# Layer 0's 16 modulation slots between the pieces of the branches' merge in place of the route; GpSimd's third half there waits until the places are counted

## What is computed

```python
mod  = silu(c) @ w_ada[i] + b_ada[i]            # 6 x 1024 values, for x
modc = silu(c_ctx) @ w_ada[i] + b_ada[i]        # the same for the context
sh1, sc1, gt1, sh2, sc2, gt2 = split(mod, 6)
...
ga, gb, gc = split(sigmoid(gates), 3)
m = ga * (ya @ w_branch[0]) + gb * (yb @ w_branch[1]) + gc * (yc @ w_branch[2])
x = x + gt1 * (m @ w_out)                        # the merge, then "out"
h2 = modulate(rmsnorm(x, g_norm2[i]), sh2, sc2)
aff = softmax(h2 @ w_router)                     # 16 experts
gate, idx = top_k(aff^T, 32)                     # each expert takes 32 tokens
x = x + gt2 * experts(h2 gathered by idx)        # w_e1, w_e3, w_e2 per expert
```

## Time and profile before

| | us |
|---|---|
| median of 3 runs | 2873.31 |
| lowest, highest | 2867.41, 2874.86 |
| profiled execution | 2874.76 |
| its span in the trace | 2872.9 |
| PE busy in the span | 2546.1 (89%) |
| DVE, ACT, POOL busy | 1053.3, 882.9, 426.6 |
| merge and out of layer 0 | about 1197 to 1440 |
| route of layer 0 | about 1440 to 1506 |
| experts of layer 0 | about 1506 to 1970 |

### The profile page before, as it was taken

One profiled execution on the slowest core, in us unless ns is written; L12 is line 12 of the kernel. 1 busy time (PEld: TensorE's weight loads), 2 busy tenths in 40 slices (PEclk: granted clock), 3 DMA queues, 4 the chain that ended last, 5 costly groups with the idle time before them and its releaser, 6 DMA issues. The chain is left out here.

```text
span 2872.9 us, 37682 instructions
## 1 busy us (share of the span) xinstructions
PE 2546.1 (89%) x15020; PEld 1781.4 (62%) x15020; DVE 1053.3 (37%) x1526; ACT 882.9 (31%) x1395; POOL 426.6 (15%) x217
## 2 busy tenths in 40 slices
PE   7999989999999999799988888887897997888887
PEld 6888878899997678588842222224776983222222
DVE  4547633246754434544340011114455651000001
ACT  4565533344443344332331000002334441000001
POOL 0430017670000221100310000000232011000000
PEclk8999999999999999899989999999998998999999
DMA  5434327764543121322279999996212447999996
GB/s 212 162 133 162 118 77 302 295 229 161 183 151 130 59 70 45 147 103 92 99 310 410 421 421 421 421 421 262 103 60 84 174 176 328 422 421 421 421 421 272
DMA packets 92891, 669.49 MB, mean 233 GB/s; under 512 B 10288, under 2 KB 10432, under 8 KB 12736
## 3 DMA queue, kind: packets, MB, share of 16 engines
q1 hardware_dynamic: 90256, 654.63, 57.7%
q0 software_dynamic: 2208, 11.56, 1.1%
q10 hardware_dynamic: 272, 1.05, 0.1%
HBM read 666.13 MB, written 1.06 MB: 232 GB/s over the span
## 5 line engine op out<-in xcount | busy, mean ns | idle before, releaser
L2429 PE MATMUL ps<-ring,WK 128*64 128x512 f32 x2984 | 703.2, 604 | 116.0 <-DMA ring<-in_stream 91.6
L545 PE MATMUL ps<-A,piece_hi 128*128 128x256 f32 (+1 forms) x1952 | 621.0, 318 | 30.0 <-ACTq L442 7.2
L546 PE MATMUL ps<-A,piece_hi 128*128 128x256 f32 (+1 forms) x1952 | 607.7, 311 | 0.0
L547 PE MATMUL ps<-A,ring_lo 128*128 128x256 f32 (+1 forms) x1952 | 607.3, 311 | 0.0
L2429 PEld LDWEIGHTS ps<-ring,WK 128*64 128x64 f32 x2984 | 192.2, 137 | 591.2 <-DMA ring<-in_stream 284.5
L455 ACT ACTIVATE piece_hi<-ring 128x1024 fp32r<-128x1024 f32 x378 | 393.2, 1054 | 206.5 <-DVEq L571 105.2
L545 PEld LDWEIGHTS ps<-A,piece_hi 128*128 128x128 f32 x1952 | 380.0, 195 | 70.2 <-issue 36.8
L466 POOL TENSOR_TENSOR ring_lo<-ring,piece_hi 128x1024 fp32r<-128x1024 f32 x123 | 311.7, 2546 | 689.8 <-ACT piece_hi L455 689.6
L464 DVE TENSOR_TENSOR ring_lo<-ring,piece_hi 128x1024 fp32r<-128x1024 f32 x255 | 317.2, 1248 | 256.2 <-ACT piece_hi L455 255.7
L546 PEld LDWEIGHTS ps<-A,piece_hi 128*128 128x128 f32 x1952 | 380.5, 195 | 18.3
L547 PEld LDWEIGHTS ps<-A,ring_lo 128*128 128x128 f32 x1952 | 379.7, 194 | 18.3
(11 more groups left out here) (271 smaller groups left out, 2661.3 us busy)
## 6 DMA issues: line engine op xcount, KB each, us to landing
ring<-in_stream SPq DMA_DIRECT2D x610, 1024.0 KB, 11.7
WK<-in_ahead SPq DMA_DIRECT2D x5, 1024.0 KB, 11.6
WK<-in_na_bias POOLq DMA_DIRECT2D x2, 2048.0 KB, 8.0
hi_place<-in_ahead SPq DMA_DIRECT2D x4, 1024.0 KB, 13.9
WK<-cum_scratch POOLq DMA_DIRECT2D x1, 2048.0 KB, 10.8
A_place<-in_ahead SPq DMA_DIRECT2D x2, 1024.0 KB, 16.9
const<-in_const SPq DMA_DIRECT2D x1, 1235.0 KB, 10.4
WK<-in_x SPq DMA_DIRECT2D x1, 1024.0 KB, 5.1
```

The costliest lines, as they stand in the source:

```text
L545: nc.tensor.matmul(out_, l[0], r[0], start=first, stop=False)
L546: nc.tensor.matmul(out_, l[0], r[1], start=False, stop=False)
L547: return nc.tensor.matmul(out_, l[1], r[0], start=False, stop=last)
L2429: last = nc.tensor.matmul(ps[64 * n:64 * n + 64, bank, :], lhs, piece[:, n * 512:n * 512 + 512], start=(k == 0), stop=(k == DC - 1))
```

## The change

Layer 1's modulation slots 8 to 23 move, in the stream and in the programs of PE and DVE, from the route of layer 0 into its merge: one behind each of the first 16 pairs of pieces, with the turns of slots 8, 16 and 24. The merge of layer 0 rotates over banks 0 to 5, and `out` and the route over all 8. SyncE issues the four ahead loads behind the first six expert slots, where it did so 10 slots earlier in the stream. In the route POOL's subtraction for m = 2 also waits for `placed`; the one for m = 3 is queued behind it.

```diff
@@ _mark
         if layer == 0:
             steps(1, range(DC), 0)
-        at += MERGE_PIECES
-        if layer == 0:
-            steps(1, range(DC, 3 * DC), 0)
+            steps(1, range(DC, DC + 18), 2)
+            at += MERGE_PIECES - 36
+        else:
+            at += MERGE_PIECES
@@ merge_pe, merge_dve
-        def merge_pe(pe, cur, branches, kc, n, ada=None):
+        def merge_pe(pe, cur, branches, kc, n, ada=None, slot=0):
             yh, yl = y_split(kc, n)
-            slot = 0
@@ route_pe (and the same kind of lines in route_dve)
-            if ada:
-                ada_pe(pe, cur, 1, step[-1])
...
-                    if ada and at % 2 == 1 and at < 12:
-                        ada_pe(pe, cur, 1, 18 + at // 2)
@@ route_pool
                 pool.wait_ge(h2_hi, cur.base("h2") + m + 1)
+                if m == 2:
+                    pool.wait_ge(placed, cur.base("route") + 1)
@@ sync
-            run(R, EXPERTS_AT[0] // 2 - 4)
+            run(R, EXPERTS_AT[0] // 2 + R)
             come_ahead(0)
-            run(EXPERTS_AT[0] // 2 - 4, EXPERTS_AT[1] // 2 + 4)
+            run(EXPERTS_AT[0] // 2 + R, EXPERTS_AT[1] // 2 + 4)
@@ programs of PE, ACT and DVE
+                cur.set_ring(range(NB) if layer else range(6))
+                merge_pe(pe, cur, 3, BC, n, ada=None if layer else 1, slot=DC)
                 cur.set_ring(range(NB))
-                merge_pe(pe, cur, 3, BC, n)
                 out_pe(pe, cur, n)
-                cur.set_ring(range(6) if layer == 0 else range(NB))
@@ _stream
             ...
+                if l == 0:
+                    ada(1, DC + 6 * n + 3 * h + 2)
         fm(x["w_out_2"][l], 0, D)
-        if l == 0:
-            for slot in range(DC, 3 * DC):
-                ada(1, slot)
```

More of the change, by code:

```diff
@@ L1753, in merge_act, with merge_dve @@
             cur.add("merge", 2 * branches + 1)
-        def merge_dve(dve, cur, steps, branches, kc, n, y, ada=None):
+        def merge_dve(dve, cur, steps, branches, kc, n, y, ada=None, slot=0):
             yh, yl = y_split(kc, n)
-            slot = 0
             def behind_two():
@@ L2234, in row_order, with route_pe @@
             return [(m, h) for h in range(2) for m in range(tt)]
-        def route_pe(pe, cur, st, ada):
+        def route_pe(pe, cur, st):
             tt = 2 * st
             wr = p2("w_router", 0, DC * 32).rearrange("p (k e) -> p k e", k=DC)
-            step = {-1: 8, 3: 9, 5: 10}
             b = cur.bank()
@@ L2260, in route_pe @@
                         token_rows(i)
-                if ada and k in step:
-                    ada_pe(pe, cur, 1, step[k])
             last.then_inc(bank_full[b], 1)
@@ L2268, in route_pe @@
                 token_rows(i)
-            if ada:
-                ada_pe(pe, cur, 1, 11)
             pe.wait_ge(affinities, cur.base("route") + 1)
@@ L2274, in route_pe @@
                 token_rows(i)
-            if ada:
-                for slot in range(12, 16):
-                    ada_pe(pe, cur, 1, slot)
             pe.wait_ge(placed, cur.base("route") + 1)
             bank_parts(pe, cur, [(P, m * 64, 64, [(PLACE[0:64, m * P:(m + 1) * P], ident[0:64, 0:64])]) for m in range(2)], turn=True)
-            if ada:
-                for slot in range(16, 18):
-                    ada_pe(pe, cur, 1, slot)
             pe.wait_ge(onehot, 2 * cur.base("route") + 1)
@@ L2338, in route_pool, with route_dve @@
             cur.add("route", 1)
-        def route_dve(dve, cur, steps, st, ada):
+        def route_dve(dve, cur, steps, st):
             tt = 2 * st
@@ L2400, in route_dve @@
             skip_banks(cur, 1)
-            if ada:
-                ada_dve(dve, cur, 1, 16)
             for s in range(st):
@@ L2711, in _ @@
                 norm_spread_pe(pe, cur, n)
-                route_pe(pe, cur, n // T, ada=layer == 0)
+                route_pe(pe, cur, n // T)
                 barrier(pe, cur)
@@ L2807, in _ @@
                 barrier(act, cur)
+                cur.set_ring(range(NB) if layer else range(6))
+                merge_act(act, cur, 3, BC, n, Y2, None)
                 cur.set_ring(range(NB))
-                merge_act(act, cur, 3, BC, n, Y2, None)
                 out_act(act, cur, n, SQ_MIX)
                 table(steps, ACT.Sqrt)
-                cur.set_ring(range(6) if layer == 0 else range(NB))
                 barrier(act, cur)
@@ L2906, in _ @@
                 barrier(dve, cur)
+                cur.set_ring(range(NB) if layer else range(6))
+                merge_dve(dve, cur, steps, 3, BC, n, Y2, ada=None if layer else 1, slot=DC)
                 cur.set_ring(range(NB))
-                merge_dve(dve, cur, steps, 3, BC, n, Y2)
                 out_dve(dve, cur, n, gain=lambda c, s: MOD[:, layer * MODC + 2 * DC + c, s:s + 1])
                 gmod_dve(dve, steps, "g2", 6 * layer + 4)
-                cur.set_ring(range(6) if layer == 0 else range(NB))
                 barrier(dve, cur)
                 main_norm_dve(dve, cur, steps, n, lambda c, s: gmod[:, c, s:s + 1], split=False)
-                if layer == 0:
-                    ada_dve(dve, cur, 1, 8)
-                route_dve(dve, cur, steps, n // T, ada=layer == 0)
+                route_dve(dve, cur, steps, n // T)
                 barrier(dve, cur)
@@ L3082, in _stream @@
                     fm(w, lo + 256 * j, lo + 256 * j + 256)
+                    if l == 0:
+                        ada(1, DC + 6 * n + 3 * h + j)
                 fm(x["w_branch_2"][l, n], h * 512, h * 512 + 512)
+                if l == 0:
+                    ada(1, DC + 6 * n + 3 * h + 2)
         fm(x["w_out_2"][l], 0, D)
-        if l == 0:
-            for slot in range(DC, 3 * DC):
-                ada(1, slot)
         for e in range(EXPERTS):
```

8 lines of the change are left out of this document (removed).

## The result

| | before | after |
|---|---|---|
| median of the paired runs (20 each), us | 2872.35 | 2878.17 |
| lowest, highest | 2865.62, 2877.96 | 2872.74, 2882.09 |
| ratio | | 1.0019, 95% interval 1.0012 to 1.0027 |

The changed kernel is 5.8 us slower by the medians, 0.19% by the ratio, and so within 0.3%. Two more comparisons gave 1.0030 (1.0019 to 1.0040) and 1.0026 (1.0016 to 1.0037).

A forecast was written before the change was run, and what follows sets the result against it. PE was taken to bound the merge, a chain of mostly DVE steps the route, and transfers the experts. Merge 21.4 us lost, route 12.6 gained, experts 0.5 lost: 9.3 us later, 2882.6 us, range 2875.5 to 2888.

The forecast's parts named there:

- The merge: Layer 0's PE-bound merge: 16 inserted slots at 1.17 us plus three turns make it 21.4 us longer.
- rival (4): Route gives more or merge asks less, a slot's joint hiding under longer products: 2878.7 us, chance 0.22.
- The front: Route's start through router and softmax: without slots between the router's matmuls, 0.4 us gained, at most 0.95.
- The count: DVE's count in the route: with POOL's halves three and four held back, the comparison starts 4.0 us earlier.
- The comparison: DVE's L2396 in the route, now beside POOL's third half: keeps its 2.48 us.
- rival (2): New wait at DVE's comparison against POOL's halves three and four: 2.2 us more, 2884.8 us, chance 0.08.
- The gather: PE's gather in the route: starts 7.3 us earlier, takes 18.1 us instead of 22.97, so 4.9 us gained.
- The tail: Route's end before the experts: PE's last turn falls away and it starts behind ACT's copies, 0.4 us gained.
- The experts: Start of the experts' stage: first slot comes free later if PE's clock is low, 0.5 us lost.
- rival (5): Experts' weights come earlier if the ring was not full: 2867.7 us with all six missing slots, chance 0.03.
- Rival (3): TensorE loses its filler; low clock covers router, more of the gather and first experts: 3.6 us, 2886.2 us, chance 0.15.

The follow-up runs named there:

- hidden_ten: Changed kernel with only slots 8 to 13 in the merge, the other ten in PE's route waits, ahead loads issued as before: 2865.03 us, 0.9975; repeated 2864.62 us, 0.9981.
- slots_in_waits: Kernel before plus POOL's wait, all 16 slots still in the route but placed mostly in PE's waits, two in the gather: 2869.83 us, ratio 0.9990.
- sixteen_behind: slots_in_waits with the four ahead loads issued behind the first six expert slots: 2872.01 us, ratio 0.9993.
- slots_only: Changed kernel without POOL's wait for the places, so only the slots are moved: 2887.31 us, ratio 1.0055 against the kernel before.
- wait_only: Kernel before with POOL's third half waiting for the places, all 16 slots left in the route: 2873.73 us, ratio 1.0010.
- hidden_twelve: hidden_ten with two more slots in the route, 12 ahead of the router and 13 ahead of the softmax's turn: 2871.40 us, ratio 0.9997.
- twelve_behind: hidden_twelve with the four ahead loads issued behind the first six expert slots: 2870.09 us, ratio 0.9991.
- slots_again: The kernel of slots_only (changed kernel without POOL's wait) once more beside the kernel before: 2885.08 us, ratio 1.0046.
- warm_route: Changed kernel with filler matmuls, read by nobody, in PE's waits of layer 0's route: 2877.74 us, ratio 1.0023 against the kernel before.

## Why the prediction was right or wrong

**The merge, +21.4: right in kind, a little small.** At the full clock it was 262.9 - 240.7 = +22.2 us, 16 x 1.22 + 3 x 0.89. The price per slot was 1.22 and not 1.17 us: nothing of the joint hides under the longer products, as rival (4) had it. PE idled nowhere in the merge, so six banks and DVE's copies cost nothing. hidden_ten shows the same price with six slots.

**The front, 0.4 gained: measured 1.2, and its size hangs on where the low level falls.** The logits come 13.93 us behind the norm's sums where they came 15.12. I had capped the gain at 0.95 us by ACT's idle time, but left out that the part ahead of ACT could be shorter too: the norm's spread took 0.62 us at the full clock (1456.48) where before had 1.09 (1443.75). In the profiles in which the spread took 1.09 us, the logits came 15.1 to 15.2 us behind the sums with slots in the front (before, slots_in_waits, sixteen_behind) and 14.9 to 15.0 without (slots_only, hidden_ten): 0.1 to 0.3 us for the slots. In those in which it took 0.62, they came at 15.5 with slots (wait_only) and at 13.9 to 14.1 without (six profiles): some 1.5 us. So the gain is 0.1 to 1.6 us by the level's place, and my 0.4 was one value out of that; before had the one case and after the other. A slot there need not cost: with slot 12 alone ahead of the router, the logits came at 13.2 (hidden_twelve, twelve_behind), and the low level was over 7.9 us behind the sums, where it was over after 10.2 to 13.7 in the other profiles.

**The count, 4.0 gained: right.** From the marking's end to the comparison are 2.04 us where there were 6.05. The scan and the mask agree with the Trainium skill's rule of the lock (SBUF — State Buffer, "SBUF: two separate sides").

**The comparison, 2.48: right, rival (2) falls.** It kept its time beside POOL's half of 1476.82. By the same section of the Trainium skill it should be free too, with one input in PSUM.

**The gather: start 7.3 earlier, measured 8.2; 4.9 shorter, measured 5.9.** The start is the front's 0.8 more. Its length was forecast as 15.0 + 3.05; it is 14.8 at the full clock (hidden_ten) and 2.3 for the low level. Windows of 2 us from the gather's start in after (columns as above):

```profile
1480.00:1482.00 2.00, 2.00 (x5) 1.59 (x6) 0.00 (x0) 0.12 (x1) 1.49 (x1) 0.50 0.00 0
1482.00:1484.00 2.00, 2.00 (x6) 1.54 (x5) 0.41 (x1) 0.48 (x1) 0.00 (x0) 0.50 0.00 0
1484.00:1486.00 2.00, 2.00 (x8) 1.57 (x8) 0.29 (x2) 0.60 (x1) 0.00 (x0) 0.84 0.00 0
```

The level is the lower of the two (1.2 GHz) at the gather's start, behind PE's waits of 6.67 and 2.57 us. With (1 - 0.84) x 2 x 2 us = 0.6 us of it in the last window it ends at about 1484.6, after 4.9 us, where layer 1's gather had 6.1. I had taken the size from one stretch in another place.

**The tail, 0.4 gained: measured 1.6.** From the gather's end to the first expert were 7.67 us and are 6.03. The turn of `PH` took 3.36 us at the low clock in before and 1.97 now (1500.02). I had looked only at the turn that fell away and not at the level of that row.

**The experts, 0.5 lost: measured 0.4 to 0.9.** Their stage kept its length, so rival (5) falls, as the DMA share of 0.01 had said.

**The sum.** Route 12.6 forecast, 15.7 measured; merge 21.4 and 22.2; experts 0.5 and 0.4 to 0.9. The net is +6.9 to +7.6 us in the three profiles where I had +9.3, and the runs gave +5.5 to +8.6. The steps were the right ones. The terms that were mis-sized are the three that hang on TensorE's level (front, gather, tail), each too small by 0.8 to 1.2 us, all on one side. The merge's 0.8 us more went the other way, so the net is nearer to the forecast than the route is, and that part is luck. I had put 0.52 on more than 0.3% slower and 0.45 on the band in which the time lies. Rival (4) has the time, with half its mechanism: the route gave more, the merge did not ask less. Rival (3) falls in its result. The level was low over the router in after (granted clock 0.50 from 1458 to 1464), but it was so in before too (0.50 and 0.58 from 1446 to 1450). Its first 32 matmuls took 2.96 us where they took 1.88 because PE, with no slot between, came to them earlier and went at the pace of ACT's rows. The level was low at the gather's start as well, but `PH` and the experts were at the full clock.

**What the change misses.** It pays 1.22 us for each slot, where the waits of the route held ten for 0.2 to 1.3 us of route in sum, and the slots filled PE's thin rows besides.

## What to carry to other kernels

Filler work costs its full time in a stage where an engine is never idle, and next to nothing ahead of a wait that another engine ends; so move it into waits before moving it out of the stage, and count how many the transfers can feed there. Before freeing an engine in a stage, look at what is late next: here the same 4 us of DVE were worth 4 to 5 us without slots in the route and nothing with them, since slot 20 had not landed. When executions differ by more than the change is worth, compare stages at equal clock and check their sum against the timed ratio.

## What the hardware showed that I had not expected

- The same work took 1189 to 1198 us up to the merge in fourteen profiles, and TensorE's level was low there for 82 to 113 us. The profiled executions of after happened to be early in all three (1189.3, 1190.8, 1190.7 us), of slots_only and slots_again, which differ from it in one wait behind that point, less so (1197.5 and 1194.9). Whether anything but chance is in that is open.
- The low level at the gather's start follows the rows ahead of it and repeats to 0.1 us: 4.8 to 5.0 us in three profiles of after, none in warm_route and in the two of hidden_ten. In the front it did not repeat: the norm's spread took 0.62 us in some profiles of like kernels and 1.09 in others.
- A load that waits on SyncE's queue holds back loads that could go: 8.09 us of PE in hidden_twelve and 0 in hidden_ten. The load in question waits for a slot of the route in the one and for a slot of `out` in the other.
